# The up weights of a mixture-of-experts block in four transfers of 2 MB instead of eight of 1 MB

## What is computed

```python
logits = t @ w_router + b_router                 # 512 x 32
top_val, top_idx = lax.top_k(logits, 4)
gate = softmax(top_val)
# for each expert e and the tokens xb that chose it:
h = xb @ w_mlp1[e] + b_mlp1[e]                   # 1024 -> 2048, the up product
glu, lin = split(h); glu = min(glu, 7); lin = clip(lin, -7, 7)
a = glu * sigmoid(1.702 * glu) * (lin + 1)
y = a @ w_mlp2[e] + b_mlp2[e]                    # 1024 -> 1024, the down product
# out[token] += gate * y
```

## Time and profile before

| what | value |
|---|---|
| median of three executions | 1666.54 us |
| the profiled execution | 1666.67 us, span 1664.8 us |
| busy share of the span | PE 86%, DVE 45%, POOL 25%, ACT 25% |
| moved by DMA | 480.22 MB, mean 288 GB/s over the span |
| weight loads of the experts | 384 of 1024.0 KB, median 22.6 us from issue to landing |
| granted TensorE clock, mean | 0.957 |

### The profile page before, as it was taken

The page is one execution under the profiler, slowest core; times in us unless marked ns, Lnnn a source line. Parts: engine busy times, 40 slices in busy tenths (PEclk is TensorE's granted clock), DMA queues, the critical chain, the costliest instruction groups (busy, mean ns, idle before and its releaser), DMA issues. The chain is left out here.

```text
span 1664.8 us, 35552 instructions
## 1 busy us (share of the span) xinstructions
PE 1432.3 (86%) x13229; PEld 749.9 (45%) x13230; DVE 742.9 (45%) x1824; ACT 410.3 (25%) x747; POOL 412.2 (25%) x253
## 2 busy tenths in 40 slices
PE   5899989598997788999998799798788798898973
PEld 3788866366775233344433334233333333343321
DVE  6899966899205423233223322243223322233223
ACT  3442224555223111211121112111111112112112
POOL 4444556412551012111111121111211121111211
PEclk8999999799998889999999999999899999999997
DMA  4232321011338599999999999999999999999995
GB/s 149 89 101 90 100 89 51 26 39 41 118 125 368 209 327 386 381 398 399 396 381 395 397 393 391 387 397 398 389 383 395 396 395 389 389 397 399 391 385 210
DMA packets 103873, 480.22 MB, mean 288 GB/s; under 512 B 9921, under 2 KB 22465, under 8 KB 71073
## 3 DMA queue, kind: packets, MB, share of 16 engines
q1 hardware_dynamic: 85024, 451.47, 69.1%
q0 software_dynamic: 17664, 26.09, 7.3%
q10 hardware_dynamic: 1152, 2.24, 0.4%
HBM read 460.36 MB, written 19.40 MB: 288 GB/s over the span
## 5 line engine op out<-in xcount | busy, mean ns | idle before, releaser
L1020 PE MATMUL bank<-big,ring 128*32 128x512 f32 x4992 | 576.5, 613 | 96.8 <-issue 49.7
L1020 PEld LDWEIGHTS bank<-big,ring 128*32 128x32 f32 x4992 | 156.0, 112 | 482.7 <-issue 402.6
L948 POOL DMA_INDIRECT acc<-mix,sidx x96 | 149.6, 1558 | 830.6 <-ACT mix L981 819.1
L1042 PE MATMUL bank<-big,mix 128*32 128x256 f32 x4992 | 281.4, 380 | 7.5 <-DMA big<-in_d_w 7.4
L1042 PEld LDWEIGHTS bank<-big,mix 128*32 128x32 f32 x4992 | 156.1, 110 | 118.5 <-DMA big<-in_d_w 13.9
L1164 DVE TENSOR_TENSOR ring<-bank,b 128x512 f32<-128x512 f32 x96 | 66.1, 688 | 232.5 <-PE bank L1020 217.4
L972 ACT ACTIVATE ring<-ring 128x256 f32<-128x256 f32 x96 | 40.0, 416 | 499.8 <-DVE ring L1166 499.8
L439 PE MATMUL bank<-mix_r,sm_r 128*128 128x512 f32 x344 | 140.9, 410 | 15.4 <-POOL uT_r L235 9.9
L677 DVE SCALAR_TENSOR_TENSOR bank<-big,chan,bank 128x512 f32<-128x512 f32 x224 | 148.2, 752 | 0.0
L230 POOL TENSOR_TENSOR ring_r<-ring,sm_r 128x1024 fp32r<-128x1024 f32 x43 | 104.3, 2428 | 128.5 <-ACT sm_r L300 128.5
L439 PE MATMUL bank<-mix_r,ring_r 128*128 128x512 f32 x344 | 136.1, 396 | 0.0
(11 more groups left out here) (254 smaller groups left out, 1602.1 us busy)
## 6 DMA issues: line engine op xcount, KB each, us to landing
big<-in_d_w SPq DMA_DIRECT2D x384, 1024.0 KB, 22.6
ring<-in_d_dense SPq DMA_DIRECT2D x67, 512.0 KB, 3.3
xT<-in_d_xT SPq DMA_DIRECT2D x4, 512.0 KB, 8.9
uT<-in_d_x SPq DMA_DIRECT2D x1, 2048.0 KB, 9.7
u_rows<-xT SPq DMA_DIRECT2D x4, 512.0 KB, 17.0
acc<-uT SPq DMA_DIRECT2D x4, 512.0 KB, 3.6
uT<-acc SPq DMA_DIRECT2D x4, 512.0 KB, 5.2
out_rows<-xT SPq DMA_DIRECT2D x4, 512.0 KB, 2.9
```

The lines of the kernel that those rows point to most:

```text
L948: pool.indirect_dma_start(out=t.d_acc4, out_offset=bass.IndirectOffsetOnAxis(ap=t.sidx[:, g:g + 1], axis=0), in_=t.ysb[:, g, :], in_offset ...
L1020: mm = pe.matmul(halves(bank[g][c * G:(c + 1) * G, :], FC), t.xe[:, k, g * G:(g + 1) * G], cols, start=(k == 0), stop=(k == KB - 1), tile_ ...
L1042: mm = pe.matmul(bank[PY[g % 2]][c * G:(c + 1) * G, 0:FC], t.aT[:, g, x, b * G:(b + 1) * G], t.w2[:, b, x, c * FC:(c + 1) * FC], start=(b ...
```

## The change

The host lays the up weights out anew, so that for a pair of blocks (2q, 2q+1) the two 8 KB rows that one partition takes stand next to each other in memory. A pair is loaded by one transfer of 2 MB: in each partition one run of 16 KB instead of 8 KB. There is one landing semaphore for a pair and one release for a pair. `K_EACH` goes from 5 to 4, so that the blocks taken group by group begin with a pair. The loads of `t.w2` are unchanged.

```diff
-K_EACH = 5
+K_EACH = 4
+PAIRS = KB // 2
...
-            for k in range(KB - 2):
-                sp.dma_start(t.w1[:, k, :], t.d_w1[0, k * P:(k + 1) * P, :]).then_inc(t.s_w1[k], 16)
+            for q in range(PAIRS - 1):
+                sp.dma_start(t.w1[:, 2 * q:2 * q + 2, :], t.d_w1[0, q]).then_inc(t.s_w1[q], 16)
...
-                for k in range(KB):
-                    sp.wait_ge(t.s_w1used, i * KB + (k + 1 - KB))
-                    sp.dma_start(t.w1[:, k, :], t.d_w1[bass.ds(e, 1), k * P:(k + 1) * P, :].rearrange("a p n -> (a p) n")).then_inc(t.s_w1[k], 16)
+                for q in range(PAIRS):
+                    sp.wait_ge(t.s_w1used, i * PAIRS + (q + 1 - PAIRS))
+                    sp.dma_start(t.w1[:, 2 * q:2 * q + 2, :], t.d_w1[bass.ds(e, 1), q].rearrange("e p a n -> (e p) a n")).then_inc(t.s_w1[q], 16)
...
                 for k in range(K_EACH):
-                    pe.wait_ge(t.s_w1[k], i * 16 + 16)
+                    if k % 2 == 0:
+                        pe.wait_ge(t.s_w1[k // 2], i * 16 + 16)
                     for g in range(groups):
                         mm = up(k, g)
-                    mm.then_inc(t.s_w1used, 1)
+                    if k % 2:
+                        mm.then_inc(t.s_w1used, 1)
...
                     for k in range(K_EACH, KB):
-                        if g == 0:
-                            pe.wait_ge(t.s_w1[k], i * 16 + 16)
+                        if g == 0 and k % 2 == 0:
+                            pe.wait_ge(t.s_w1[k // 2], i * 16 + 16)
                         mm = up(k, g)
-                        if g == last:
+                        if g == last and k % 2:
                             mm.then_inc(t.s_w1used, 1)
...
-        "d_w1": a["w_mlp1"][0], "d_w2": a["w_mlp2"][0],
+        "d_w1": a["w_mlp1"][0].reshape(E, PAIRS, 2, P, 2 * D).transpose(0, 1, 3, 2, 4), "d_w2": a["w_mlp2"][0],
```

More of the change, by code:

```diff
@@ L204, in _ @@
             sp.wait_ge(t.s_prod, used(N_CHUNK - 1))
-            for k in range(KB - 2, KB):
-                sp.dma_start(t.w1[:, k, :], t.d_w1[0, k * P:(k + 1) * P, :]).then_inc(t.s_w1[k], 16)
+            sp.dma_start(t.w1[:, KB - 2:KB, :], t.d_w1[0, PAIRS - 1]).then_inc(t.s_w1[PAIRS - 1], 16)
             for j in range(TT):
@@ L1071, in work @@
                 if groups < NG:
-                    pe.wait_ge(t.s_w1used, i * KB + KB)
+                    pe.wait_ge(t.s_w1used, i * PAIRS + PAIRS)
                     pe.sem_inc(t.s_up, 1)
@@ L1160, in gated @@
                 else:
-                    dve.wait_ge(t.s_w1used, i * KB + KB)
+                    dve.wait_ge(t.s_w1used, i * PAIRS + PAIRS)
                 if g == 0:
@@ L1465, in build @@
         t.s_w = sems("s_w", NSLOT)
-        t.s_w1 = sems("s_w1", KB)
+        t.s_w1 = sems("s_w1", PAIRS)
         t.s_w2 = sems("s_w2", 4)
```

## The result

The changed kernel takes 1651.8 us (median of 4 runs), the kernel before 1666.4 us on the same chip: ratio 0.9916, 95% interval 0.9898 to 0.9934, so 14.6 us less (11 to 17). The forecast was 1659.6 us with a range from 1654 to 1671: right in sign, short by half in size, and 2 us outside its range. The profiled execution is 1652.12 us with a span of 1650.3, against 1664.8 before.

The account below looks back on a forecast made before the run. From 650 us on the DMA engines set the mixture's pace. Row and completion savings -10.5, last-expert tail +2.5 and later start +1.0 summed to -7.0 us, giving 1659.6 us, with a range from 1654 to 1671.

Parts of the forecast that it names:

- Rows of other queues: Scatter and gather rows alternating with 16 KB weight rows: they come later, DMA time unchanged, delay covered; costed at nothing.
- the landing of a pair: PE waits for both blocks of up weights; at the last expert two more units follow the last landing, +2.5 us.
- The fixed part per row: Up-weight loads: each row carries about 9.4 ns, so 16 KB rows save -9.3 us over 31 experts.
- Rivals A and C: A: 16 KB rows no faster than 8 KB, 1668.8 us, chance 0.17; C: 4 KB rows' pace, up to 1685, 0.06.
- Completions: Up-weight loads: four completion records per engine and expert fewer, estimated at -1.2 us.
- The release of a pair: First reload of the mixture waits for block 1, so DMA starts 3.9 us later, mostly hidden; +1.0 us taken.
- K_EACH 4: First group of a three-group expert completes after 16 units instead of 18; nothing on the path waits, 0 us.
- Delay of the scatters: DVE's wait for the scatters (line 1201) comes some 5 to 7 us later after an expert's start.
- Rival B: Software queue falls behind, DVE and PE wait for scatters and gather; about 1684 us, or 1670 to 1675; chance 0.10.
- Rival D: DMA gain larger, up to -16 us, with the tail hidden: -13 to -15 us, 1652 us; chance 0.07.
- The pace itself: Time per expert in the mixture: about 33.4 us, from 33.75 by the count of issued loads.

Follow-up runs that it names:

- before_2g: The kernel before with every expert run with two groups, the third group's tokens of 14 experts left out; 1656.9 us, ratio 0.9941 to the kernel before.
- after_2g: The changed kernel with every expert run with two groups, the third group left out; 1642.4 us, ratio 0.9850 to the kernel before.
- before_2g_lategather: before_2g with the next gather issued only when PE has released five of the eight up blocks; 1649.5 us, ratio 0.9903 to the kernel before.
- pair8: The changed kernel with the weights in DRAM as in the kernel before, so rows stay 8 KB; 1666.8 us, ratio 1.0002 to the kernel before.
- after_w2rows: The changed kernel with the down weights in rows of 8 KB instead of 4 as well; 1653.0 us, ratio 0.9924 to the kernel before.
- after_keach6: The changed kernel with K_EACH 6, only the last pair of blocks taken group by group; 1654.3 us, ratio 0.9927 to the kernel before.
- before_lategather: The kernel before, two or three groups per expert, with the gather issued when five up blocks are released; 1689.3 us, ratio 1.0137 to it.
- keach4: The kernel before with K_EACH 4 instead of 5 alone; 1665.7 us, ratio 0.9997 to the kernel before.

## Why the prediction was half right and half wrong

**What failed.** The step "Rows of other queues", which ended in "The DMA time doesn't change" and "I cost it at nothing". The sum of the forecast was -7.0 us, and this term, entered as 0, holds most of what is missing to -14.6. An estimate for the full kernels, from the marks and the last expert: the pace gives 31 x 0.48 = -14.9 us for -10.5, the start +1.3 for +1.0, the landing of a pair +2.0 for +2.5, and the last up weights land 2.7 us sooner behind mark 31 (below), for nothing in the forecast. These add up to -14.3 us. The table has the same for the kernels with two groups, where PE can't blur it (us, each against its partner with rows of 8 KB):

| | to mark 5 | pace x 26 | behind mark 31 | span |
|---|---|---|---|---|
| 16 KB rows, no software queue | +1.3 | -7.9 | +3.0 | -3.7 |
| 16 KB rows, scatters, no gather | +1.0 | -8.2 | +3.5 | -3.7 |
| 16 KB rows, whole | +0.4 | -12.0 | -4.0 | -15.6 |
| 8 KB rows, gather moved | +4.4 | -8.4 | -4.1 | -8.2 |
| full kernels, after against before | -1.1 | -12.4 | -1.0 | -14.5 |

The first two lines hold the forecast's own terms, and they come to -3.7, not -7.0, since the start and the end cost more in these kernels (below). The third has 4 us more in the pace and 7 us more at the end, and has them only if the gather is there. The fourth shows that the gather's place by itself can do both, with no row changed. The 7 us are read from one execution each, but the medians agree: 14.5 us for 5.5. The chain is this. One row of the software queue goes through per row of weights, which the prediction had read from the earlier trace rows. With 16 KB between them the scatters of an expert take 13.9 instead of 10.1 us, and the gather behind them falls out of the up weights into the down weights, where its turn waits for 4 KB instead of 8 or 16. Its first packet comes 2.0 us behind the first down row in after and 1.6 us ahead of it before. It is in flight 3.16 instead of 3.59 us with two groups, 3.13 instead of 3.39 in the full kernels, and the last up weights land sooner. At the last expert, the last up landing stands 9.8 us behind mark 31 in before_2g, 3.2 in after_2g and 4.9 in before_2g_lategather. In the full kernels it is 5.3 and 2.6 us. The prediction asked of the delay only whether someone waits for it. It didn't ask which transfers the delayed one would then run beside. The longer scatters aren't the only thing that can move the gather: in pair8 they take 10.2 us, but start 8.8 us ahead of the first down row instead of 11.9, and most gathers fall beside down weights too.

after_w2rows fits this. With no rows of 4 KB left, the gather has no cheap place: it is in flight for 4.06 us, for 3.13 in after, and most of what fewer rows save is lost there. That a gather is longer in flight beside larger rows is what the turns lead one to expect, but they aren't all of it: beside 4 KB rows alone it takes 2.53 us in before_2g_lategather and 3.50 in after_keach6. Why the rate beside it stays near 330 GB/s whatever the rows is not shown.

**The fixed part per row.** Right. -9.3 us for 31 experts was forecast; the two pairs without gather give 31 x 0.305 = 9.5 and 31 x 0.316 = 9.8 us, and the stretch alone shows 428 GB/s where 428 to 431 was named. Rivals A and C, at 424 GB/s and below, are out.

**Completions, -1.2 us.** Too high, and not separated. The pairs without gather leave at most 0.02 us per expert for them, 0.6 us in all; the 0.14 of pair8 goes with the moved gather.

**The landing of a pair.** Right. +2.5 us forecast. From last landing to down product: +2.0 in the full kernels, +1.7, +1.7 and +2.6 in the three pairs with two groups, +3.2 in pair8. That a unit takes longer behind a wait is seen again: 7.05 / 6 = 1.18 us, at the granted clock of 0.72 shown here, the changed kernel from 1609 to 1615 us:

```profile
1609.00:1615.00 6.00, 6.00 (x44) 1.66 (x47) 2.21 (x6) 0.42 (x1) 0.00 (x0) 0.72 1.03 369
```

**The release of a pair.** Nearly right for the full kernels, too low for those with two groups. +1.0 us was taken. The first reload is issued at 567.51 us, for 564.50:

```profile
567.51 15.77 SPq L921 DMA_DIRECT2D big<-in_d_w  x4
```

The bytes are 0.3 us behind at 664 us in the full kernels, with three experts' saving of about 1 us already in it: the start cost some 1.3 us. In the pairs with two groups 0.4 to 1.3 us are left at mark 5, with five experts' saving in it: 2 to 3 us, most of the delay of the issue.

**K_EACH 4.** Right, nothing.

**Delay of the scatters.** Right in size: forecast 5 to 7 us, seen 4.6 in the expert shown and 3.7 on average, with PE hardly touched. Rival B didn't come. That it was near is shown by after_w2rows (the first waits for the gather) and before_lategather (its price).

**Rival D** had the right size (1652 us) and the wrong reason: a larger gain of the rows with the tail hidden. The rows by themselves gained what was forecast and the tail wasn't hidden; that D's number fits is luck.

**The pace itself.** The forecast named 33.4 us per expert, from 33.75 by the count of issues. By bytes the pace before was 34.07, and it is 33.59 now: the count of issues was 1% off, and the difference, -0.34, should have been -0.48.

**What stays open.** In after_2g 7.5 us of the end are unexplained by the forecast's terms (+3.5 without gather, -4.0 with it), and the moved gather alone shows 4.1 of them; how much of the rest is chance a single profiled execution of each kernel can't tell, as the 3.5 us of keach4 warn. The gather's place by itself was tried with two groups alone: in the full kernel the same edit moved it elsewhere. So its share there is carried over from the pairs. In before_2g_lategather PE waits for the gather in the first five experts (15.6 us in 5 waits), which is most of its +4.4 to mark 5, so the place itself may be worth more than 7.3 us.

## What to carry to other kernels

Where DMA sets the pace, a delayed transfer that nobody waits for may still cost or save time: it will run beside other transfers, so ask beside which, and what row size its queue then takes turns with. Here a gather in rows of 4 KB cost least beside the shortest rows of the other queue; for the 1 KB rows of the scatters no such effect was seen. Moving it by a fixed point in the program is safe only while the lead of the loads stays the same. The fixed part per row, read from two row sizes in the trace, carried to a third and a fourth within the error.

## What the runs showed of the hardware

- Rates of weights alone, by my count in stretches of 1 us: 410 GB/s in rows of 4 KB, 422 in 8, 428 in 16, 432 in 32. That is a straight line per byte plus 9 to 10 ns a row.
- The two queues of an engine take turns row by row at every size tried: 310 to 321 at 8 KB, 182 to 179 at 16 KB, 87 to 96 at 32 KB. How long a software row waits for its turn therefore grows with the other queue's row.
- While a gather is in flight, all 16 engines together move 323 to 336 GB/s on average of each kernel, whether the weights beside it come in rows of 4, 8 or 16 KB.
- Holding the gather back until five of the eight up blocks are used was worth 7.3 us in one kernel, where it put the gather beside the down weights, and cost some 23 us in its sibling with more PE work, where PE waited for it and it came to stand beside the up weights.
